# A stretch of products of zeros ahead of TensorE's first turns in a two-layer decoder step

## What is computed

```python
def trunk(x, p, pos, h0_re, h0_im, build_kv, w):
    for i in range(DEPTH):                       # 2 layers
        hn = rmsnorm(x, w['norm_mix_g'][i])
        if i < N_A_LAYERS:                       # layer 0: diagonal state-space mixer
            o, hr, hi = s5_mixer(hn, ...)
        else:                                    # layer 1: sparse attention on shared K/V
            o = nsa_mixer(hn, pos, kv, ...)
        x = x + o
        x = x + swiglu(rmsnorm(x, w['norm_ffn_g'][i]), w['ffn_w_gate'][i],
                       w['ffn_w_up'][i], w['ffn_w_down'][i])
        gate = jax.nn.sigmoid(rmsnorm(x, w['norm_ple_g'][i]) @ w['ple_w_gate'][i])
        x = x + gate * (p[i] @ w['ple_w_proj'][i])
        if i == N_A_LAYERS - 1:
            kv = build_kv(x)                     # K/V rows, and compression of the paged cache
    return rmsnorm(x, w['norm_final_g']), ...
```

## Time and profile before

| | |
|---|---|
| median of three runs | 3227.9 us |
| profiled execution, span from first to last instruction | 3225.4 us |
| mean granted TensorE clock over the span | 0.994 |
| TensorE busy | 3178.8 us (99%) |
| VectorE, ScalarE, GpSimd busy | 1996.9, 1553.3, 519.6 us |

### The profile page before, as it was taken

One profiled execution on the slowest core, in us unless ns is written; L12 is line 12 of the kernel. 1 busy time (PEld: TensorE's weight loads), 2 busy tenths in 40 slices (PEclk: granted clock), 3 DMA queues, 4 the chain that ended last, 5 costly groups with the idle time before them and its releaser, 6 DMA issues.

```text
span 3225.4 us, 68754 instructions
## 1 busy us (share of the span) xinstructions
PE 3178.8 (99%) x27708; PEld 3040.6 (94%) x27708; DVE 1996.9 (62%) x2283; ACT 1553.3 (48%) x1929; POOL 519.6 (16%) x476
## 2 busy tenths in 40 slices
PE   7999999999999999999999999999999999999998
PEld 6999899999999999999999997866999999999998
DVE  7888888865655544555675546465655554455566
ACT  4555655644544444444554533354554444444454
POOL 5666666600000000000000006000000000000000
PEclk8999999999999999999999999999999999999999
DMA  6445555466566556565556559898556555666553
GB/s 183 146 149 161 170 160 157 139 182 187 176 189 178 185 184 192 176 187 184 180 182 183 183 183 313 284 354 263 184 181 184 175 189 182 183 176 189 183 179 130
DMA packets 384388, 608.39 MB, mean 189 GB/s; under 512 B 52537, under 2 KB 144986, under 8 KB 383882
## 3 DMA queue, kind: packets, MB, share of 16 engines
q1 hardware_dynamic: 351738, 539.06, 53.8%
q10 hardware_dynamic: 29392, 60.86, 5.6%
q0 software_dynamic: 3024, 5.22, 0.5%
HBM read 594.83 MB, written 26.94 MB: 193 GB/s over the span
## 4 chain that ended last, share of the span: by engine, by line
PE 94%; DVE 3%; DMA 1%; ACT 1%; issue 0%; POOL 0%; ACTq 0%; SPq 0%; DVEq 0%; POOLq 0%
PE psum L429 23%; PE psum L431 23%; PE psum L430 23%; PE psum L1081 4%; PE psum L1083 3%; PE psum L1082 3%; PE psum L1060 3%; PE psum L2436 2%; PE psum L2446 1%; PE psum L2484 1%; PE psum L1138 1%; PE psum L1164 1%; PE psum L2301 1%; PE psum L2327 1%; DMA taps_first<-in_cmp_k_w 1%; PE psum L2315 0%
## 5 line engine op out<-in xcount | busy, mean ns | idle before, releaser
L396 DVE TENSOR_TENSOR w_rest<-w_raw,w_head 128x1024 fp32r<-128x1024 f32 x776 | 973.1, 1265 | 944.4 <-ACT w_head L392 943.5
L392 ACT ACTIVATE w_head<-w_raw 128x1024 fp32r<-128x1024 f32 x776 | 909.8, 1183 | 944.6 <-PE psum L431 935.4
L429 PE MATMUL psum<-act_head,w_head 128*128 128x264 f32 x4224 | 1205.0, 285 | 1.6 <-DVE act_rest L2894 1.6
L431 PE MATMUL psum<-act_head,w_rest 128*128 128x264 f32 x4224 | 1200.6, 284 | 0.0
L430 PE MATMUL psum<-act_rest,w_head 128*128 128x264 f32 x4224 | 1199.7, 284 | 0.0
L429 PEld LDWEIGHTS psum<-act_head,w_head 128*128 128x128 f32 x4224 | 821.6, 195 | 2.4 <-issue 1.9
L430 PEld LDWEIGHTS psum<-act_rest,w_head 128*128 128x128 f32 x4224 | 822.2, 195 | 0.1
L431 PEld LDWEIGHTS psum<-act_head,w_rest 128*128 128x128 f32 x4224 | 821.6, 195 | 0.0
L429 PE MATMUL psum<-hid_head,w_head 128*128 128x264 f32 x1408 | 400.6, 284 | 0.0
L431 PE MATMUL psum<-hid_head,w_rest 128*128 128x264 f32 x1408 | 399.9, 284 | 0.0
L430 PE MATMUL psum<-hid_rest,w_head 128*128 128x264 f32 x1408 | 399.5, 284 | 0.0
(11 more groups left out here) (433 smaller groups left out, 4007.9 us busy)
## 6 DMA issues: line engine op xcount, KB each, us to landing
w_raw<-in_ffn_w_gate SPq DMA_DIRECT2D x176, 512.0 KB, 4.1
w_raw<-in_ffn_w_up SPq DMA_DIRECT2D x176, 512.0 KB, 4.5
w_raw<-in_ffn_w_down SPq DMA_DIRECT2D x176, 512.0 KB, 3.8
w_raw<-in_cache_cmp_k SPq DMA_DIRECT2D x256, 128.0 KB, 2.6
w_raw<-in_cache_cmp_v SPq DMA_DIRECT2D x256, 128.0 KB, 2.6
w_raw<-in_ssm_w_glu SPq DMA_DIRECT2D x64, 512.0 KB, 4.5
w_raw<-in_ple_w_gate SPq DMA_DIRECT2D x64, 512.0 KB, 4.2
w_raw<-in_kv_w SPq DMA_DIRECT2D x48, 512.0 KB, 3.8
```

The source lines that it names most:

```text
L392: nc.scalar.activation(pairs(WH, u), tiles_of(RAW, u), ACT.Copy).then_inc(head_done, 1)
L396: nc.vector.tensor_tensor(pairs(WL, u), tiles_of(RAW, u), pairs(WH, u).bitcast(F32), ALU.subtract).then_inc(rest_done, 1)
L429: nc.tensor.matmul(o, wh, head, start=k == 0, stop=False)
L431: last = nc.tensor.matmul(o, wl, head, start=False, stop=k == UK * kunits - 1)
```

## The change

VectorE sets a tile `WARM` of 2112 float32 columns to zero ahead of the `ONES` tile, and TensorE, once `ones_done` is there, runs `warm_pe` in front of everything else: 201 fp32r products of that tile with itself, into PSUM banks 1 and 2, whose results nobody reads. 169 of them have 264 columns, 8 each 256, 240, 200 and 128. They come in 22 groups: forward and reversed column order, weights contiguous, by every second or every fourth column, moving tiles that begin at other columns, one bank or two in turn, accumulated or each on its own. `WARM` lies at `hn_at`.

```diff
+    WARM = sb("warm", [P, 8 * T], F32R, at=hn_at)
...
+    def warm_pe(pe):
+        pe.wait_ge(ones_done, 1)
+
+        def weights(m, first=0, step=1):
+            if step > 1:
+                tile = WARM[:, step * P * (m // step % (8 // step)):step * P * (m // step % (8 // step) + 1)]
+                tile = tile.rearrange("p (c e) -> p c e", e=step)[:, :, m % step]
+            else:
+                tile = WARM[:, m % 4 * P + first:m % 4 * P + first + P]
+            return tile
+
+        def run(count, n, lhs=weights, first=0, back=False, stride=1, banks=1, fresh=False):
+            for m in range(count):
+                at = first(m) if callable(first) else first
+                o, r = PSUM[:, 2 - m % banks, 0:n], WARM[:, 1024 + at:1024 + at + stride * n:stride]
+                if back:
+                    o, r = o[:, ::-1], r[:, ::-1]
+                last = nc.tensor.matmul(o, lhs(m), r, start=fresh or m < banks, stop=fresh or m >= count - banks, skip_group_check=True)
+            return last
+
+        run(32, T)
+        run(8, 2 * P)
+        run(8, 240)
+        run(8, 200)
+        run(8, P)
+        run(8, T, back=True)
+        run(8, T, back=True, lhs=lambda m: weights(m, step=2))
+        run(8, T, back=True, lhs=lambda m: weights(m, step=4))
+        run(8, T, back=True, first=32)
+        run(8, T, back=True, first=64)
+        run(8, T, back=True, banks=2)
+        run(9, T, back=True, lhs=lambda m: weights(m // 3 * 2 + m % 3 // 2, step=2), first=lambda m: 512 * (m % 3 == 1))
+        run(8, T, banks=2)
+        run(8, T, fresh=True)
+        run(8, T, first=8)
+        run(8, T, first=16)
+        run(8, T, first=32)
+        run(8, T, first=64)
+        run(8, T, back=True, first=16)
+        run(8, T, lhs=lambda m: weights(m, first=16))
+        run(8, T, stride=2)
+        run(8, T, lhs=lambda m: weights(0))
...
+        warm_pe(pe)
         pe.wait_ge(ld["const"], 16)
         pe.wait_ge(par_dve, 1)
...
     def start_dve(dve):
+        nc.vector.memset(WARM[:, :].bitcast(F32), 0.0)
         nc.vector.memset(ONES[:, :], 1.0)
```

## The result

Three runs of the changed kernel gave 3244.71, 3245.22 and 3247.87 us, median 3245.22, against 3227.90 before: the ratio is 1.0056 (95% interval 1.0042 to 1.0070), 0.56% slower. The profiled execution's span went from 3225.4 to 3242.9 us, 17.5 more; the medians are 17.3 apart.

What follows compares the result with a forecast made beforehand. TensorE, busy in nearly the whole span, was taken to bound the kernel. First turn 19.35 us later, less 1.5 returned, adds 17.85 us; 3227.9 + 17.9 = 3245.8 us, range 3240.5 to 3251.5.

Steps and rivals of the forecast that it cites:

- The hole and the start: TensorE stands still until 10.15 us; VectorE's added memset takes 1.82 us, and products start at 3.0 us.
- The price of a product: Each of the 201 added products at TensorE's start takes 0.1206 us at full clock, 24.2 us in all.
- the strided reads: Sixteen added products with weights of every fourth or moving tile of every second column: 0 to 1.9 us extra, 0 taken.
- The slow part: The first 5.0 us of added products run at 1.2 GHz, 0.22 us each, costing 2.3 us more.
- The sum of the products: At TensorE's start, 24.2 + 2.3 = 26.5 us, ending at 29.5 us; first turn 19.35 us later.
- What comes back: Behind the first turn, faster turns and clock effects return 0 to 4.5 us; 1.5 us taken.
- The slow stretch at 59 us: From 59 to 66 us, 27 slow-clock products cost 2.5 us; may be met or missed, 0 in the sum.
- The sign of being wrong: Four signs named, among them the distance between the two timelines changing between 60 us and the end.
- 3263: Rival: the clock never rises on the added products, which end at 45.7 us; total 3263.4 us; chance 0.04.
- no instruction came late: Rival on TensorE's added instructions: a block missed for some 5 us in the products, total 3250.8 us; chance 0.04.
- the start absorbed nothing: Rival at the start: the products' slip is covered by what is given back, total 3227 us; chance 0.02.
- Dear groups: Rival: strided reads, odd starts and groups of one cost half more, some 60 products, 3.6 us, 3249.4 total; chance 0.05.

Runs made afterwards that it cites:

- e1_idle: The changed kernel without the products, VectorE setting the WARM tile 16 times in a row so TensorE starts late with an unraised clock: 3255.75 us.
- e2_short: The changed kernel with only 36 products of 264 columns, meant to end inside the hole: 3226.51 us, ratio 0.9999 to the kernel before.
- e4_plain: The changed kernel with contiguous tiles in place of weights of every fourth column and the moving tile of every second: 3243.63 us.
- e8_strides: The changed kernel with 128 products in place of the 201: 32 of 264 columns, then eight of each strided or differently sized form; one run, 3244.25 us.
- e3_double: The changed kernel with all 22 groups of products run twice, 402 products: 3271.73 us.
- e7_raised: As e1_idle, with the later 15 memsets on another tile and 46 products between the 13th memset and the first turn: 3252.88 us.
- e10_hold: As e2_short, with 14 more products of 256 columns in TensorE's wait for the first normed chunk: 3227.50 us, ratio 0.9999 to the kernel before.

## Why the prediction was right, point by point

The forecast was 3245.8 us and the median 3245.2. The direction, the mechanism and the size held. That the number is only 0.6 us off is luck: the spans' distance was 19.35 + 0.29 (start) + 1.84 (products) - 2.56 (return) - 1.4 (attention) = 17.5, against 19.35 - 1.5 = 17.85, four terms off that nearly cancelled.

**The hole and the start.** Right. The memset took 1.82 us as worked out; the products began at 3.29 and not 3.0 us, because VectorE's first instruction started at 1.26 us and not at 0.85. The change's trace, e1_idle and e2_short all have 1.26; what delays it isn't shown.

**The price of a product.** The step that bounded the strided reads "by nothing below and by a doubling above" and took nothing was wrong, and the upper bound was nearly exact: 0.237 us in both groups, 1.87 us in all; what the earlier trace rows covered was only weights of every second column. e4_plain and e8_strides show it as the tile's price. The reasoning from one operand to the other was the mistake: a row on weights says nothing of the moving tile, for which every second column is already dear, and a row on every second column says nothing of every fourth. The page of the Trainium skill that I had set beside it, Advanced Engine Details and Errata, section "SBUF Cachelines", was right on the weights of every fourth column (0.237 against 0.120), and its pairs would have let the moving tile of every second column go free; there the measurement decides, 0.240. The plain groups of 264 columns lay between 0.120 and 0.125 us, with a dearer first product at a change of form (0.17) and 0.136 in the last group, whose last product is followed by the first turn only after 0.21 us. The estimate of 0.1125 us by the Trainium skill's page TensorE: Matmul & The Clock Gate, section "Back-to-back issue gap", stayed out of reach for a product of 264 columns, as the rows had said.

**The slow part.** Right in kind and size: products at 0.220 us and a rise 4.6 us after the first (5.0 taken). In e4_plain it was 5.7 and in e3_double 5.9 us after it, so this term alone moves the time by half a microsecond from one execution to the next.

**The sum of the products.** 28.34 us against 26.5. With the late start, the first turn slipped by 21.48 and not 19.35.

**What comes back.** I had taken 1.5 us, out of 0 to 4.5. It was 2.56 by 90 us (that VectorE's full chain keeps what the first half gains was the right half of the step), and e1_idle against e7_raised shows that 2.3 of it is the raised clock under the turns, through VectorE's earlier copies. The step that made it smaller said that a fall of the clock under the second half of x would eat the gain. As it was worded, a fall "as early relative to the first turn" as before (17.7 us behind it) would hardly have met those chunks, which ended 17.6 us behind it before. But the fall came sooner (10.5 us behind it), and it did raise the distance, from 18.95 at the second page turns to 20.6 at the third; but by the sum of the squares it is back at 19.04. That step let TensorE's second eight chunks set the pace, and they stand beside GpSimd's parts, which had begun 18.94 us late and end later. So the gain of the first half stays, and the loss of the second doesn't count. This reading rests on the eight traces' distances and was not isolated by a run of its own. The rest, 1.4 us in the attention, is a fall of the clock that comes and goes between executions; the sum had no such term.

**The slow stretch at 59 us.** It was priced at 2.5 us, left out of the sum and put into the upper end of the range. In the change it came again as long as before (76.2 to 83.1 us by the clock's record), so it gave nothing either way, but the price was too high: where it was half as long it was worth 0.2 us, because TensorE then waits for VectorE (e10_hold).

**The sign of being wrong.** The prediction named one that did occur: the distance changed between 60 us and the end, from 19.92 to 18.92 by 90 us and by another 1.4 in the attention. It shows that the sum lacked a term there, not that its mechanism was wrong.

**The rivals.** The clock rose under products of zeros, so 3263 is out; no instruction came late, even in 55 us; the start absorbed nothing. "Dear groups" was half true, with 16 products and not 60, and at twice the price. That the products would not fit into the hole was right: 6.9 of 28.3 us lie in it.

## What to carry to other kernels

Work put ahead of an engine's first real task is free only up to the moment at which that task would have begun; behind it each microsecond costs one, less what the raised clock gives back, in a program that this engine bounds, however small the share looks. Raising the clock ahead of it is worth what the slow stretch costs on the engine that paces it (here 2.3 us, and under 1 us once the loads pace it), so the stretch should end with the hole. And price each operand of a product from a row of its own: a stride that is free on one side was double on the other.

## What the runs showed of the hardware that I had not expected

- A moving fp32r tile of every second, third or fourth column takes 0.234 to 0.242 us for 264 columns where a contiguous one takes 0.120; weights of every second column cost 3 ns, of every third 51 ns, of every fourth or eighth 117 to 122 ns.
- As long as new weights are loaded for each product, it takes about 0.11 us however few columns move (groups of 32 to 240 columns: 0.101 to 0.112, and 0.112 for 64 columns behind the first product).
- The clock rose under turns alone: in e1_idle a chunk of x took 0.82 us until 45 us and 0.52 from 52 us on, with nothing but turns in between. The Trainium skill's page TensorE: Matmul & The Clock Gate, section "Part 4: PE-mode transpose", has it that the full clock doesn't engage in transposes; this trace disagrees.
- A semaphore between two memsets of VectorE cost 0.51 us each time, against no gap between those that follow freely.
